# A tuned two-block language-model kernel: residual turns that transpose the tokens before they are normed

## The chip, the cores and the metric

The kernel is one program on one core of a Trainium2 chip. A core has a matrix engine (TensorE, PE in the profile; its weight loads are the row PEld), a vector engine (VectorE, DVE), an activation engine (ScalarE, ACT), GpSimd (POOL) and a queue engine that issues transfers (SyncE, SP). They share an on-chip memory (SBUF) and eight accumulation banks (PSUM, `bank[0]` to `bank[7]` in the code). Each engine works its own list in order and waits for the others on semaphores. The metric is the device time of one execution in microseconds (us), lower is better.

## The reference

256 tokens of width 1024 go through two blocks. What this change touches is in the second one:

```
def rms_norm(x, g):
    xf = xf * lax.rsqrt(jnp.mean(xf * xf, axis=-1, keepdims=True) + EPS)
    return (xf * g.astype(F32)).astype(x.dtype)

h = first_block(...)                   # ends: h + peer_ffn(...), then rmsnorm(h, g_final)
h = h + hgrn2_mixer(rms_norm(h, hg_norm), ...)      # q, f, i, g = split(x @ w_in, 4)
h = h + conv_ffn(rms_norm(h, ffn_norm[0]), ...)     # gate, val = split(x @ w_up, 2)
k, v = split(rms_norm(h, kv_norm) @ w_kv, 2)
h = h + swa_sink_attention(rms_norm(h, attn_norm), k, v, w_q, sinks, w_o)
h = h + conv_ffn(rms_norm(h, ffn_norm[1]), ...)
out = rms_norm(h, final_norm)
```

In the mixer q becomes `silu(q)`, f becomes `lower_bound + (1 - lower_bound) * sigmoid(f)`, k is one minus that, and eight levels of a gated linear attention follow. In the feed-forward, gate goes through a causal convolution over three tokens and a silu, and is multiplied with val. The norm's factor `rsqrt(mean(x*x) + EPS)` is one number for each token, its gain one number for each channel.

## The kernel before, in words

**Slabs.** All weights come as a stream of 524 slabs of 128 x 1024 floats. SP loads slab n into a ring of four (`RING = 4`). ACT rounds it to `whi` (L237, `split_hi`), DVE takes the rest `wlo = raw - whi` (L245, `split_lo`), both three slabs ahead (`AHEAD = 3`) of the slab that PE multiplies. Activations are split likewise into `xhi` and `xlo`, and a product is three matmuls (hi by hi, hi by lo, lo by hi). `up` (L273 to L275) multiplies a slab with the turned activations into one bank, 24 matmuls; `up_halves` (L294, L298) does it with eight wide and eight short ones; `down` (L338 to L340) adds 12 wide matmuls onto the residual banks 4 to 7; `up_wide` (L330 to L332) gives token-major outputs. An `up` into a bank waits (`up_evac`) until its last content has been taken out.

**A turn.** Between two layers stands a turn. `down_last` finishes the four residual banks one by one. DVE adds them to `h` (`add`, L510; `h` is token-major: two times 128 tokens by 1024). ACT squares each quarter with a sum (L624), takes the root (L637), DVE the reciprocal (L522), and `nt = h * factor` is written in pieces by DVE (`scale`, L527) and ACT (L661). PE turns `nt` by 16 transposes (`turn_pe`, L680 and L686). ACT reads the turned banks times the gain into `xhi` (`turn_hi`, L704), DVE into `xlo` (`turn_lo`, L713), in eight pieces each; the first `up` after the turn starts as soon as the first piece of `xlo` is there. There are six turns: T_WQ, T_HG (before the mixer, where the first block's final norm and the mixer's norm stand in a row, so that also `UT = h * g_final` is formed, L516), T_FF0, T_ATT, T_FF1 and T_OUT (the output).

**The mixer.** 16 `up`s in four banks give f (the first eight, taken out by ACT with a sigmoid, L2068) and q (the last eight: four taken out by DVE copies, L2226, four by ACT with a silu, L2082). DVE forms `forget` (L2179, L2182) and the residual (L2188), then scans the logarithms (L2233), subtracts (L2218) and forms differences (L2209, L2211). When all 16 are taken out (`up_evac`), PE may overwrite the banks with the token-major products (`up_wide`), between which the levels of the linear attention stand (L1979).

**The feed-forward.** For each of 22 tiles PE does an `up_halves` for the gate, one for val, and a `down`. Gate: ACT copies one half of its bank (L2396), DVE adds the other (L2439), ACT begins the convolution (L2399), DVE ends it (L2444). Val: ACT copy (L2404), DVE add (L2455), after the silu (L2407) DVE multiplies (L2458). The order of each engine's list is written out by hand; only SP and the ring decide when a slab arrives.

Of the kernel before, what the change touches and what calls it, by code (L numbers as in the profile page):

```python
# [131 lines left out]
def build(nc, t):  # L132
    ctx = ExitStack()
    with ctx:
# [148 lines left out]
        def up_halves(pe, n0, u0, i, r, U, uU=None, x_ready=None):  # L283
# [210 lines left out]
        TRT, TRS, TR1 = tiny[:, 42:44], tiny[:, 44:46], tiny[:, 46:48]  # L494
# [24 lines left out]
        def root_turned(dve, a, tt):  # L519

            dve.wait_ge(turn_rt, 2 * a + tt + 1)
            nc.vector.reciprocal(TRS[:, tt:tt + 1], TRT[:, tt:tt + 1]).then_inc(turn_rs, 1)  # L522
            dve.wait_ge(turn_rs, 2 * a + tt + 1)

        def scale(dve, a, c0, c1):
            src = UT if a == T_HG else h
            nc.vector.tensor_scalar(nt[:, c0:c1], src[:, c0:c1], TRS[:, c0 // D:c0 // D + 1], None, ALU.mult)\  # L527
                .then_inc(turn_nt, 1)
# [11 lines left out]
        def turn_dve(dve, a):  # L540
# [5 lines left out]
            if a == T_ATT:  # L546
                add(dve, a, 2)
                first_mean(dve, a)
                add(dve, a, 3)
                root_turned(dve, a, 0)  # L550
            else:
                first_mean(dve, a)
                add(dve, a, 2)
                root_turned(dve, a, 0)
                add(dve, a, 3)
# [7 lines left out]
        def mean_h(dve, tt, k0, k1, count):  # L563

            dve.wait_ge(turn_ss, SS_BASE[T_HG] + count)
            nc.vector.scalar_tensor_tensor(out=TW[:, tt:tt + 1], in0=ss(k0), scalar=EPS, in1=ss(k1),
                                           op0=ALU.add, op1=ALU.add).then_inc(turn_v, 1)

        def mean_u(dve, tt, k, count):

            dve.wait_ge(turn_ss, SS_BASE[T_HG] + count)
            dve.wait_ge(turn_v, V_BASE[T_HG] + 2 * tt + 1)
            nc.vector.scalar_tensor_tensor(out=TV[:, tt:tt + 1], in0=TW[:, tt:tt + 1], scalar=EPS, in1=ss(k),
                                           op0=ALU.mult, op1=ALU.add).then_inc(turn_v, 1)

        def turn_dve_gained(dve, row):

            a = T_HG  # L580
# [36 lines left out]

        def turn_act(act, a):
# [15 lines left out]
            def root(tt, k):
                act.wait_ge(turn_v, V_BASE[a] + VALUES[a] // 2 * (tt + 1))
# [4 lines left out]
            if a == T_HG:  # L640
                square(0, 0)
                square(1, 1)
                square_u(0, 2)
                square(2, 3)
                square_u(1, 4)
                root(0, 4)
                square(3, 5)
                square_u(2, 6)
                square_u(3, 7)
                root(1, 7)  # L650
            else:
                square(0, 0)
                square(1, 1)
                root(0, 1)
                square(2, 2)
# [2291 lines left out]
```

## Time and profile before

| | us |
|---|---|
| median of 3 runs | 1697.04 (1697.02 to 1697.94) |
| the profiled execution's own time | 1697.7 |
| its span in the profile | 1695.9 |
| PE busy | 1664.8 (98%) |
| DVE busy | 1286.7 (76%) |
| ACT busy | 1031.6 (61%) |

The profile is of one execution. Its engine rows count work, not waiting; what ends the program is read from the chain of waits and from which engine has no gaps. The engines' views in order of time show when an instruction started, how long it took, and in brackets how long its engine had been idle and who ended that.

### The profile page before, as it was taken

What the parts mean: (1) busy time and instruction counts of PE and PEld (TensorE: products, weight loads), DVE (VectorE), ACT (ScalarE), POOL (GpSimd) and SP (SyncE); (2) the same over time, 40 slices, a digit from 0 to 9 for tenths busy, and PEclk for the clock granted to TensorE, in tenths of its full rate; (3) what the DMA queues carried; (4) which work ended last, traced back from release to release, by engine and by line L of the source; (5) the groups of instructions that cost most, each with busy time, mean ns of one, the idle gap of its engine ahead of it and who ended that gap; (6) DMA issues with size and microseconds to landing.
All of it is one profiled execution on the core that took longest, in us unless ns stands there. A gap on an engine that the chain in (4) does not pass through costs nothing.

```text
span 1695.9 us, 34377 instructions
## 1 busy us (share of the span) xinstructions
PE 1664.8 (98%) x10835; PEld 1505.4 (89%) x10835; DVE 1286.7 (76%) x2365; ACT 1031.6 (61%) x1628; POOL 114.5 (7%) x102
## 2 busy tenths in 40 slices
PE   8999999999999999999999999999999999999998
PEld 7998889999999999988888888898888888878886
DVE  6866773899977777777777777789777777977776
ACT  7766655776556666654545455665576657766665
POOL 0024300344100000000000000100000000000000
PEclk9999999999999999999999999999999999999999
DMA  5543355777765555477787777542445564246563
GB/s 204 179 150 97 117 204 179 201 225 224 242 202 175 170 174 178 164 232 243 239 277 240 244 241 240 184 152 78 158 162 188 194 189 153 100 152 196 190 193 112
DMA packets 113405, 315.62 MB, mean 186 GB/s; under 512 B 12640, under 2 KB 44768, under 8 KB 112960
## 3 DMA queue, kind: packets, MB, share of 16 engines
q1 hardware_dynamic: 112032, 310.43, 56.5%
q0 software_dynamic: 848, 4.00, 0.7%
q8 instruction: 36, 0.59, 0.1%
q10 hardware_dynamic: 464, 0.40, 0.1%
q14 instruction: 25, 0.20, 0.0%
HBM read 296.43 MB, written 18.35 MB: 186 GB/s over the span
## 4 chain that ended last, share of the span: by engine, by line
PE 94%; DVE 2%; ACT 2%; issue 1%; DMA 1%; ACTq 0%; DVEq 0%; POOL 0%; POOLq 0%
PE bank L273 12%; PE bank L274 12%; PE bank L275 12%; PE bank L338 11%; PE bank L339 11%; PE bank L340 11%; PE bank L294 9%; PE bank L298 5%; PE bank L1522 3%; PE bank L1979 2%; PE bank L330 1%; PE bank L332 1%; PE bank L331 1%; DMA iota<-in_iota 1%; DVE h L510 0%
## 5 line engine op out<-in xcount | busy, mean ns | idle before, releaser
L245 DVE TENSOR_TENSOR wlo<-raw,whi 128x1024 fp32r<-128x1024 f32 x499 | 612.4, 1230 | 132.1 <-ACT whi L237 119.6
L237 ACT ACTIVATE whi<-raw 128x1024 fp32r<-128x1024 f32 x524 | 550.1, 1052 | 19.9 <-PE bank L332 14.0
L273 PE MATMUL bank<-x,whi 128*128 128x256 f32 (+1 forms) x1728 | 506.1, 293 | 1.5 <-DVE x L713 0.7
L275 PE MATMUL bank<-x,wlo 128*128 128x256 f32 (+1 forms) x1728 | 491.1, 284 | 0.0
L274 PE MATMUL bank<-x,whi 128*128 128x256 f32 (+1 forms) x1728 | 490.5, 284 | 0.0
L273 PEld LDWEIGHTS bank<-x,whi 128*128 128x128 f32 x1728 | 330.6, 191 | 5.2 <-issue 3.6
L274 PEld LDWEIGHTS bank<-x,whi 128*128 128x128 f32 x1728 | 331.3, 192 | 0.1
L275 PEld LDWEIGHTS bank<-x,wlo 128*128 128x128 f32 x1728 | 330.3, 191 | 0.0
L338 PE MATMUL bank<-whi,yhi 128*128 128x512 f32 x816 | 319.4, 391 | 0.8 <-DVE ylo L2319 0.7
L339 PE MATMUL bank<-wlo,yhi 128*128 128x512 f32 x816 | 318.2, 390 | 0.0
L340 PE MATMUL bank<-whi,ylo 128*128 128x512 f32 x816 | 317.6, 389 | 0.0
L338 PEld LDWEIGHTS bank<-whi,yhi 128*128 128x128 f32 x816 | 153.4, 188 | 33.5 <-issue 1.2
L340 PEld LDWEIGHTS bank<-whi,ylo 128*128 128x128 f32 x816 | 153.2, 188 | 32.4
L339 PEld LDWEIGHTS bank<-wlo,yhi 128*128 128x128 f32 x816 | 153.4, 188 | 29.4
L294 PE MATMUL bank<-x,whi 128*128 128x512 f32 x704 | 177.4, 392 | 0.9 <-DVE x L713 0.7
L1606 ACT ACTIVATE yhi<-h 128x256 fp32r<-128x256 f32 x128 | 53.4, 417 | 170.5 <-PE bank L340 167.1
L294 PEld LDWEIGHTS bank<-x,whi 128*128 128x128 f32 x704 | 129.2, 188 | 27.1 <-issue 1.2
L1559 ACT ACTIVATE h<-bank 128x256 f32<-128x256 f32 x128 | 49.0, 383 | 150.0 <-PE bank L275 149.7
L1800 DVE TENSOR_TENSOR ylo<-h,yhi 128x256 fp32r<-128x256 f32 x128 | 54.4, 425 | 66.5 <-ACT yhi L1606 66.3
L298 PEld LDWEIGHTS bank<-x,wlo 128*128 128x128 f32 x704 | 96.9, 190 | 6.9
L298 PE MATMUL bank<-x,wlo 128*128 128x256 f32 x704 | 100.2, 282 | 0.0
L1755 DVE TENSOR_SCALAR h<-iota,h 128x128 f32<-128x128 f32 x256 | 76.9, 343 | 22.9 <-PE bank L1522 22.9
(321 smaller groups left out, 1718.1 us busy)
## 6 DMA issues: line engine op xcount, KB each, us to landing
raw<-in_stream SPq DMA_DIRECT2D x524, 512.0 KB, 3.6
act_spill<-h SPq DMA_DIRECT2D x124, 128.0 KB, 3.3
h<-act_spill SPq DMA_DIRECT2D x124, 128.0 KB, 3.9
h<-in_x SPq DMA_DIRECT2D x2, 512.0 KB, 4.6
arena<-in_keys POOLq DMA_DIRECT2D x1, 1024.0 KB, 6.2
h_spill<-h SPq DMA_DIRECT2D x1, 1024.0 KB, 7.6
arena<-h_spill POOLq DMA_DIRECT2D x1, 1024.0 KB, 6.9
arena<-in_g_final POOLq DMA_DIRECT2D x1, 512.0 KB, 8.8
```

The lines of the kernel that those rows point to most:

```text
L237: nc.scalar.activation(whi[:, q * 1024:(q + 1) * 1024], raw[:, q * 1024:(q + 1) * 1024], ACT.Copy).then_inc(hi_ready, 1)
L245: nc.vector.tensor_tensor(wlo[:, q * 1024:(q + 1) * 1024], raw[:, q * 1024:(q + 1) * 1024], whi[:, q * 1024:(q + 1) * 1024].bitcast(F32), ...
L273: nc.tensor.matmul(bank[b][:, 0:T], whi[:, w], xhi[:, x], start=k == 0, stop=False)
L274: nc.tensor.matmul(bank[b][:, 0:T], whi[:, w], xlo[:, x], start=False, stop=False)
L275: last = nc.tensor.matmul(bank[b][:, 0:T], wlo[:, w], xhi[:, x], start=False, stop=k == KT - 1)
L294: return nc.tensor.matmul(bank[b][:, :], whi[:, w], both, start=k == 0, stop=k == KT - 1)
L298: return nc.tensor.matmul(bank[b][:, SEQ:2 * SEQ], wlo[:, w], xhi[:, k * SEQ:(k + 1) * SEQ], start=False, stop=stop, skip_group_check=True)
L338: nc.tensor.matmul(o, yhi[:, y], whi[:, w], start=first, stop=False, skip_group_check=True)
L339: nc.tensor.matmul(o, yhi[:, y], wlo[:, w], start=False, stop=False, skip_group_check=True)
L340: return nc.tensor.matmul(o, ylo[:, y], whi[:, w], start=False, stop=True, skip_group_check=True)
L1755: nc.vector.tensor_scalar(HOT1[:, y % 2 * P:(y % 2 + 1) * P], iota[:, :], c1(I1T), c1(GT_COLS), ALU.is_equal, ALU.mult).then_inc(s("hot_a" ...
L1800: nc.vector.tensor_tensor(ylo[:, yq * SEQ:(yq + 1) * SEQ], PRD[:, yq * SEQ:(yq + 1) * SEQ], yhi[:, yq * SEQ:(yq + 1) * SEQ].bitcast(F32), ...
```

## The change

At the four turns T_HG, T_FF0, T_ATT and T_FF1 PE now transposes `h` itself (`turn_pe_late`), as soon as the adds are done. The factor is worked out behind that (`factor_dve`, `roots_act`), and PE and ACT spread it to `ROW`, one number for each token, alike in all partitions (`row_pe`: two matmuls of the factor's column with the identity, `row_act`: a copy out of bank 7). It is applied where products are taken out: in the mixer all 16 `up`s are taken out by DVE as `bank * ROW` (`taken`), and ACT does sigmoid and silu in place behind that; v and the output gate get it as ACT's scale. In the feed-forward the gate is multiplied by `ROW` after its halves are added, val is left without the factor, and the down sums get it in the add of the next turn (T_ATT and T_OUT). In the attention keys are taken out by DVE times `ROW`, values get it in ACT's copy, and of the queries it goes into the scale of the exponential, so that the distance table and the sinks are divided by it. At T_HG the gain is the product of both norms' gains, for which `g_final` is loaded once more, channel-major.

```diff
+        def turn_dve_late(dve, a, gain_name, row=None):
+            add(dve, a, 0)
+            add(dve, a, 1)
...
+            add(dve, a, 3)
+            turn_lo(dve, a, gain_name)
+        def factor_dve(dve, a):
+            dve.wait_ge(turn_ss, SS_BASE[a] + SUMS[a])
...
+                nc.vector.reciprocal(INV, ROOT).then_inc(turn_rs, 1)
+        def turn_act_late(act, a, gain_name):
...
+            square(act, a, 2)
+            turn_hi(act, a, gain_name)
+        def row_pe(pe, a):
+            pe.wait_ge(turn_rs, R_BASE[a] + 1)
+            for tt in range(TT):
+                last = nc.tensor.matmul(bank[7][:, tt * P:(tt + 1) * P], INV[:, tt:tt + 1].to_broadcast([P, P]),
+                                        ident[:, :], start=True, stop=True)
+            last.then_inc(s("row_mm"), 1)
+        def row_act(act, a):
+            act.wait_ge(s("row_mm"), a - T_HG + 1)
+            nc.scalar.activation(ROW, bank[7][:, 0:SEQ], ACT.Copy).then_inc(s("row_ready"), 1)
+        def turn_pe_late(pe, a):
+            pe.wait_ge(h_done, 4 * a + 2)
+            for x in range(KT // 2):
+                for tt in range(TT):
+                    if tt and x in (0, KT // 4):
+                        pe.wait_ge(h_done, 4 * a + 3 + x // 2)
...
         def pe_hgrn(pe):
-            turn_pe(pe, T_HG)
+            turn_pe_late(pe, T_HG)
             up(pe, N_HG, U_HG, 0, 0, 4, SEQ, x_ready=lo_base(T_HG), banks=HG_BANKS)
-            steps(pe, 15, 4, lambda i, r: up(pe, N_HG + 1, U_HG + 1, i, r, 4, SEQ, banks=HG_BANKS))
+            up(pe, N_HG + 1, U_HG + 1, 0, 0, 4, SEQ, banks=HG_BANKS)
+            up(pe, N_HG + 2, U_HG + 2, 0, 0, 4, SEQ, banks=HG_BANKS)
+            row_pe(pe, T_HG)
+            steps(pe, 13, 4, lambda i, r: up(pe, N_HG + 3, U_HG + 3, i, r, 4, SEQ, banks=HG_BANKS))
         def act_hgrn(act, chain):
...
             for j in range(8):
-                split_hi(act, N_HG + j + AHEAD, 0, 0, 4)
-                act.wait_ge(slabs_done, N_HG + j + 1 + RING)
-                nc.scalar.activation(FG[:, j * SEQ:(j + 1) * SEQ], bank[(U_HG + j) % HG_BANKS][:, 0:SEQ], ACT.Sigmoid)\
-                    .then_inc(up_evac, 1)
+                if j > 1:
+                    split_hi(act, N_HG + j + AHEAD, 0, 0, 4)
+                act.wait_ge(up_evac, U_HG + j + 1 + 2)
+                f = slice(j * SEQ, (j + 1) * SEQ)
+                nc.scalar.activation(FG[:, f], FG[:, f], ACT.Sigmoid).then_inc(s("f_sig"), 1)
         def dve_hgrn(dve, chain):
...
+            def taken(j, out):
+                if j == 0:
+                    dve.wait_ge(s("row_ready"), 1)
+                dve.wait_ge(slabs_done, N_HG + j + 1 + RING)
+                nc.vector.tensor_tensor(out, bank[(U_HG + j) % HG_BANKS][:, 0:SEQ], ROW, ALU.mult)\
+                    .then_inc(up_evac, 1)
...
-                if j < 4:
-                    if j == 0:
-                        dve.wait_ge(up_evac, U_HG + 8 + 2)
-                    dve.wait_ge(slabs_done, N_HG + 8 + j + 1 + RING)
-                    nc.vector.tensor_copy(QQ[:, j * SEQ:(j + 1) * SEQ], bank[(U_HG + j) % HG_BANKS][:, 0:SEQ])\
-                        .then_inc(up_evac, 1)
+                taken(8 + j, QQ[:, j * SEQ:(j + 1) * SEQ])
         def dve_ffn(dve, f, chain):
...
-                nc.vector.tensor_tensor(gate, gate, bank[u % 2][:, 0:SEQ], ALU.add).then_inc(s("gate_sum"), 1)
+                nc.vector.tensor_tensor(gate, gate, bank[u % 2][:, 0:SEQ], ALU.add).then_inc(up_evac, 1)
+                dve.wait_ge(up_evac, u + i * 8 + 1 + 2)
+                if first:
+                    dve.wait_ge(s("row_ready"), a - T_HG + 1)
+                nc.vector.tensor_tensor(gate, gate, ROW, ALU.mult).then_inc(s("gate_sum"), 1)
```

**Where instructions move.** VectorE's list behind the adds of T_HG, before (L527 writes the normed tokens, L713 is `turn_lo`, L245 `split_lo`, L2166 to L2173 the lower bounds, L510 the last add, L516 the gain):

```order
L510 TENSOR_TENSOR h<-arena,bank 128x512
L516 TENSOR_TENSOR arena<-h,arena 128x512
L522 RECIPROCAL tiny<-tiny 128x1
L516 TENSOR_TENSOR arena<-h,arena 128x512
L566 SCALAR_TENSOR_TENSOR tiny<-tiny 128x1
L527 TENSOR_SCALAR arena<-arena,tiny 128x512
L573 SCALAR_TENSOR_TENSOR tiny<-tiny 128x1
L527 TENSOR_SCALAR arena<-arena,tiny 128x512
L522 RECIPROCAL tiny<-tiny 128x1
L527 TENSOR_SCALAR arena<-arena,tiny 128x256 x2
L713 SCALAR_TENSOR_TENSOR x<-bank,vec,x 128x256 x8
L245 TENSOR_TENSOR wlo<-raw,whi 128x1024
```

The same place in the changed kernel (L524 is the add, L751 `turn_lo`, L530 the gain, L591 to L599 the factor, L2230 `taken`):

```order
L524 TENSOR_TENSOR h<-arena,bank 128x512
L751 SCALAR_TENSOR_TENSOR x<-bank,tiny,x 128x256 x8
L530 TENSOR_TENSOR arena<-h,arena 128x512 x2
L245 TENSOR_TENSOR wlo<-raw,whi 128x1024 x2
L2213 TENSOR_TENSOR arena<-vec 128x8
L2214 TENSOR_TENSOR arena<-vec,arena 128x8
L2215 TENSOR_TENSOR arena<-vec,arena 128x8
L591 SCALAR_TENSOR_TENSOR tiny<-tiny 128x2
L594 SCALAR_TENSOR_TENSOR tiny<-tiny 128x2
L597 TENSOR_TENSOR tiny<-tiny 128x2
L599 RECIPROCAL tiny<-tiny 128x4
L2230 TENSOR_TENSOR arena<-bank,arena 128x256 x2
```

`turn_lo` now stands right behind the last add, and the factor, four instructions, stands behind two slab splits.

VectorE's list at the end of the mixer's 16 `up`s, before (L2226 is the last of its four copies, L2233 the scans, L2218 the subtraction, L2209 and L2211 the differences):

```order
L2226 COPY arena<-bank 128x256
L2233 SCALAR_TENSOR_TENSOR arena<-vec,arena 128x256 x8
L245 TENSOR_TENSOR wlo<-raw,whi 128x1024
L2218 TENSOR_TENSOR arena<-arena 128x2048
L245 TENSOR_TENSOR wlo<-raw,whi 128x1024
L2209 TENSOR_TENSOR arena<-arena 128x8x128
L2211 TENSOR_TENSOR arena<-arena 128x8x128
L245 TENSOR_TENSOR wlo<-raw,whi 128x1024
L2209 TENSOR_TENSOR arena<-arena 128x16x64
L2211 TENSOR_TENSOR arena<-arena 128x16x64
```

The same place in the changed kernel (L2289 the scans, L2279 the subtraction, L2270 and L2272 the differences):

```order
L2230 TENSOR_TENSOR arena<-bank,arena 128x256
L2289 SCALAR_TENSOR_TENSOR arena<-vec,arena 128x256 x8
L245 TENSOR_TENSOR wlo<-raw,whi 128x1024
L2279 TENSOR_TENSOR arena<-arena 128x2048
L2230 TENSOR_TENSOR arena<-bank,arena 128x256
L245 TENSOR_TENSOR wlo<-raw,whi 128x1024
L2270 TENSOR_TENSOR arena<-arena 128x8x128
L2272 TENSOR_TENSOR arena<-arena 128x8x128
L2230 TENSOR_TENSOR arena<-bank,arena 128x256
L245 TENSOR_TENSOR wlo<-raw,whi 128x1024
L2270 TENSOR_TENSOR arena<-arena 128x16x64
L2272 TENSOR_TENSOR arena<-arena 128x16x64
```

The last four products of q, which ACT took out before, now stand in VectorE's list between the scans, the subtraction and the differences.

ScalarE's list behind T_HG in the changed kernel (L742 is `turn_hi`, L627 and L634 the squares, L673 the root, L688 `row_act`, L2113 the exponential of the lower bounds, L2119 the sigmoid):

```order
L742 ACTIVATE x<-bank,tiny 128x256 x8
L237 ACTIVATE whi<-raw 128x1024
L627 ACTIVATE arena,tiny<-h 128x512
L634 ACTIVATE arena,tiny<-arena 128x512 x2
L237 ACTIVATE whi<-raw 128x1024
L634 ACTIVATE arena,tiny<-arena 128x512 x2
L673 ACTIVATE tiny<-tiny 128x4
L688 ACTIVATE arena<-bank 128x256
L237 ACTIVATE whi<-raw 128x1024
L2113 ACT_TABLE_LOAD
L2113 ACTIVATE arena<-arena 128x16
L2119 ACT_TABLE_LOAD
```

Before, all squares and the root stood ahead of `turn_hi`, a slab split stood between the exponential and the sigmoid's table load, and one behind each sigmoid; now two sigmoids follow that load before the next split.

## Rows read from the trace of the kernel before

**Rows 1.** The page: busy time of the engines, and the chain that ended last.

```profile
PE 1664.8 (98%) x10835; PEld 1505.4 (89%) x10835; DVE 1286.7 (76%) x2365; ACT 1031.6 (61%) x1628; POOL 114.5 (7%) x102
...
PE 94%; DVE 2%; ACT 2%; issue 1%; DMA 1%; ACTq 0%; DVEq 0%; POOL 0%; POOLq 0%
```

**Rows 2.** Waits of PE: who it waited for, us in total, times, longest.

```profile
PE bank L680 <- DVE arena L527: 9.6, 5, 3.2
```

**Rows 3.** Timeline, T_HG: start, us, engine, line, operation, [idle before <-releaser].

```profile
1069.32 0.39 PE L340 MATMUL bank<-whi,ylo 128*128 128x512 f32 x1
...
1070.23 0.68 DVE L510 TENSOR_TENSOR h<-arena,bank 128x512 f32<-128x512 f32 x1
...
1072.92 1.06 PE L680 MATMUL bank<-ident,arena 128*128 128x128 f32 x8 [3.21 <-DVE arena L527]
...
1074.57 3.02 ACT L704 ACTIVATE x<-bank,vec 128x256 fp32r<-128x256 f32 x8 [0.16 <-PE bank L686]
...
1075.70 0.55 PE L273 MATMUL bank<-x,whi 128*128 128x256 f32 x1
...
1077.69 0.28 PE L273 MATMUL bank<-x,whi 128*128 128x256 f32 x1
```

**Rows 4.** Windows at T_HG, T_FF0, T_ATT: PE, PEld, DVE, ACT, POOL busy; granted clock; DMA.

```profile
1074.00:1078.00 4.00, 3.91 (x20) 3.84 (x21) 3.01 (x9) 3.84 (x10) 0.00 (x0) 0.57 0.00 0
...
1229.00:1232.00 3.00, 1.91 (x15) 1.64 (x16) 1.97 (x7) 2.22 (x6) 0.00 (x0) 1.00 0.03 5
...
1418.00:1422.00 4.00, 3.23 (x17) 3.21 (x17) 2.52 (x10) 3.31 (x10) 0.54 (x1) 0.62 0.42 147
```

**Rows 5.** Timeline behind T_HG: ACT's table load and sigmoid, PE's pace.

```profile
1081.44 1.28 ACT L2068 ACT_TABLE_LOAD   x1
1082.73 0.39 ACT L2068 ACTIVATE arena<-bank 128x256 f32<-128x256 f32 x1
...
1085.44 0.39 ACT L2068 ACTIVATE arena<-bank 128x256 f32<-128x256 f32 x1 [0.15 <-PE bank L275]
...
1088.32 0.39 ACT L2068 ACTIVATE arena<-bank 128x256 f32<-128x256 f32 x1 [1.55 <-PE bank L275]
```

**Rows 6.** Window from the mixer's sigmoids to its first token-major product, columns as in Rows 4.

```profile
1081.50:1128.30 46.80, 46.44 (x368) 45.35 (x367) 38.24 (x52) 32.48 (x38) 0.00 (x0) 1.00 0.54 175
```

**Rows 7.** Timeline, end of the mixer's `up`s: DVE's scans, ACT's last silu, PE.

```profile
1112.37 4.76 DVE L2233 TENSOR_TENSOR_SCAN arena<-vec,arena 128x256 f32<-128x256 f32 x8
...
1122.88 0.38 ACT L2082 ACTIVATE arena<-bank 128x256 f32<-128x256 f32 x1 [1.55 <-PE bank L275]
1123.32 0.50 PE L330 MATMUL bank<-whi,x 128*128 128x512 f32 x1 [0.36 <-ACT arena L2082]
...
1128.31 0.15 DVE L2236 COPY arena<-bank 128x1 f32<-128x1 f32 x1
```

**Rows 8.** Timeline, T_FF0 up to the fourth product.

```profile
1228.15 0.39 PE L340 MATMUL bank<-whi,ylo 128*128 128x512 f32 x1
1228.64 0.69 DVE L510 TENSOR_TENSOR h<-h,bank 128x512 f32<-128x512 f32 x1 [0.38 <-PE bank L340]
...
1231.53 3.02 ACT L704 ACTIVATE x<-bank,vec 128x256 fp32r<-128x256 f32 x8
...
1232.66 0.47 PE L294 MATMUL bank<-x,whi 128*128 128x512 f32 x1 [0.37 <-DVE x L713]
...
1240.99 0.41 DVE L2455 TENSOR_TENSOR arena<-arena,bank 128x256 f32<-128x256 f32 x1
1241.66 2.00 PE L294 MATMUL bank<-x,whi 128*128 128x512 f32 x8
```

**Rows 9.** Timeline, a feed-forward tile in the loop: the gate's add.

```profile
1308.81 0.42 DVE L2439 TENSOR_TENSOR arena<-arena,bank 128x256 f32<-128x256 f32 x1 [0.94 <-ACT arena L2396]
```

**Rows 10.** Timeline, T_ATT: the second `turn_lo` and the product behind it.

```profile
1430.97 3.22 DVE L713 SCALAR_TENSOR_TENSOR x<-bank,vec,x 128x256 fp32r<-128x256 f32 x8
...
1431.60 0.36 PE L273 MATMUL bank<-x,whi 128*128 128x256 f32 x1 [0.29 <-DVE x L713]
```

More of the change, by code:

```diff
@@ L508, in add @@
             q = slice(p * 512, (p + 1) * 512)
+            if a in (T_ATT, T_OUT):
+                nc.vector.scalar_tensor_tensor(out=h[:, q], in0=bank[4 + p][:, :], scalar=INV[:, p // 2:p // 2 + 1],
+                                               in1=h[:, q], op0=ALU.mult, op1=ALU.add).then_inc(h_done, 1)
+                return
             old = H_OLD if a == T_HG else h
@@ L545, in turn_dve @@
             add(dve, a, 1)
[L546 to L555, printed above, removed]
+            first_mean(dve, a)
+            add(dve, a, 2)
+            root_turned(dve, a, 0)
+            add(dve, a, 3)
             scale(dve, a, 0, D // 2)
@@ L639, in turn_act @@
             nc.scalar.activation(tiny[:, 20 + a:21 + a], tiny[:, 31:32], ACT.Sqrt)
[L640 to L655, printed above, removed]
-                square(3, 3)
-                root(1, 3)
@@ L658, in turn_act @@
-            act.wait_ge(turn_rs, 2 * a + 2)
+            square(act, a, 0)
+            square(act, a, 1)
+            root(0, 1)
+            square(act, a, 2)
+            square(act, a, 3)
+            root(1, 3)
+            act.wait_ge(turn_rs, R_BASE[a] + 2)
             if a == T_OUT:
                 act.wait_ge(turn_u, 4 + 1)
-            nc.scalar.activation(nt[:, D + 512:2 * D], (UT if a in (T_HG, T_OUT) else h)[:, D + 512:2 * D], ACT.Copy,
+            nc.scalar.activation(nt[:, D + 512:2 * D], (UT if a == T_OUT else h)[:, D + 512:2 * D], ACT.Copy,
@@ L2055, in act_hgrn @@
         def act_hgrn(act, chain):
-            turn_act(act, T_HG)
-            turn_hi(act, T_HG, "hg_norm")
+            act.wait_ge(s("hg_gain"), 1)
+            turn_act_late(act, T_HG, HG_GAIN)
             split_hi(act, N_HG - 1 + AHEAD, 0, 0, 4)
-            nc.scalar.activation(TR1[:, 0:1], TW[:, 0:1], ACT.Sqrt)\
-                .then_inc(s("x2_rt"), 1)
-            nc.scalar.activation(TR1[:, 1:2], TW[:, 1:2], ACT.Sqrt)\
-                .then_inc(s("x2_rt"), 1)
+            square(act, T_HG, 3)
+            square_u(act, 0)
+            square_u(act, 1)
+            split_hi(act, N_HG + AHEAD, 0, 0, 4)
+            square_u(act, 2)
+            square_u(act, 3)
+            roots_act(act, T_HG)
+            row_act(act, T_HG)
+            split_hi(act, N_HG + 1 + AHEAD, 0, 0, 4)
             act.wait_ge(s("lb_x"), 2)
@@ L2581, in act_attn @@
         def act_attn(act, chain):
-            turn_act(act, T_ATT)
-            turn_hi(act, T_ATT, "kv_norm")
+            turn_act_late(act, T_ATT, "kv_norm")
+            square(act, T_ATT, 3)
+            roots_act(act, T_ATT)
             split_hi(act, N_ATT - 1 + AHEAD, 0, 0, 4)
-            for k in range(2):
+            row_act(act, T_ATT)
+            for k in range(3):
                 split_hi(act, N_ATT + k + AHEAD, 0, 0, 4)
-                act.wait_ge(slabs_done, N_ATT + k + 1 + RING)
-                nc.scalar.activation(KTA[:, k * SEQ:(k + 1) * SEQ], bank[(U_ATT + k) % 2][:, 0:SEQ], ACT.Copy)\
-                    .then_inc(up_evac, 1)
-            split_hi(act, N_ATT + 2 + AHEAD, 0, 0, 4)
             turn_hi(act, T_ATT, "attn_norm", 1)
+            act.wait_ge(up_evac, U_ATT + 2 + 2)
             nc.scalar.activation(VD, bank[(U_ATT + 2) % 2][:, 0:SEQ], ACT.Copy).then_inc(up_evac, 1)
```

283 lines of the change are left out of this document (167 added, 116 removed).

## The prediction

> **What bounds the kernel now.** I read the page's busy row and the chain first: PE is busy 1664.8 of 1695.9 us, and 94% of the chain is PE [rows 1]. So a microsecond counts only where PE stops or slows. The waits of PE came second: few are left, and the largest, 9.6 us in five, is PE's transposes waiting for DVE's scaled tokens in a turn [rows 2]. Third, the timeline of each turn. At T_HG the last down matmul starts at 1069.32, the transposes at 1072.92 after 3.21 us idle, the first product at 1075.70 [rows 3]; at T_FF0 it is 1228.15 and 1232.66 [rows 8]. Fourth, the granted clock in these windows: 0.57 behind T_HG, 0.62 at T_ATT, 1.00 at T_FF0, where PE had idled less [rows 4]; a share near a half is the 1.2 GHz level instead of 2.4. Last, and this decides for me, what DVE and ACT do in the 50 us behind a turn, since the change takes work out of the turn and puts it there.
>
> **Turns, what goes.** PE needs only the adds. At T_FF0 PE is free at 1228.4. Sixteen transposes at 0.13 us (eight take 1.06, rows 3) take 2.1 us; the last add starts at 1228.64 and takes 0.69 [rows 8], and ten transposes cover it. So they end at 1230.5. ACT's `turn_hi` starts 0.37 after the third begins (1231.16 to 1231.53 before), at 1229.0 instead of 1231.53. The first product stood 1.13 behind it and would at 1230.1, but the transposes hold it to 1230.55: 2.1 us earlier than 1232.66. T_FF1 has the same form. At T_HG the gain pieces keep the last add near 1069.9 to 1070.6 (0.68, rows 3), the transposes end at 1071.65, and the first product starts at 1071.7, 4.0 us earlier. With no 3 us of idling ahead the slow clock should go too; before, the first nine product matmuls took from 1075.70 to 1077.69 [rows 3], where nine at 0.12 each take 1.08, so 0.9 more. At T_ATT the same steps give 1419.7 against 1422.0, 2.3. The four together: 4.9 + 2.1 + 2.3 + 2.1 = 11.4 us. That is what the turns offer, if nothing behind them is late.
>
> **T_FF0 and T_FF1, what is late next.** The fourth product (val of the second tile) may start only when DVE has taken the second out (L2455). Before, that was 1240.99 plus 0.41, and the product started at 1241.66 [rows 8]: no room. Now DVE does, from the end of `turn_lo` at 1233.05: the factor (0.16, ACT's root 0.3, the reciprocal 0.16 and the handovers, 0.75 in all; ACT's last square lies beside it), a split whose `whi` ACT ends at 1234.6 (to 1235.8), the gate's add (0.4), a wait on itself and the product with `ROW` (0.55), a split (to 1238.3, ACT's `row_act` is ahead of its `whi`), the convolution (1.0), a split (1.15) and the val add (0.4): 1240.9. PE is ready at 1239.3 (two row matmuls, 0.3, included), stands 1.6 us, and starts at 1240.95. Of 2.1 us 0.7 stay. Bounds: 0 and 2.1. I take 0.7, since each piece has a row's duration.
>
> **T_ATT.** In the last tile before it ACT's `whi` split now falls ahead of the val copy, so the last adds come 0.3 later; I included that. Behind it DVE takes out two key products (0.4 each) that ACT took, after waiting for `ROW`. The second `turn_lo` then starts at 1430.3, where it started at 1430.97 and PE followed at 1431.60 [rows 10]: 0.6 to 0.7 us stay, taken 0.6. Bounds: -0.5 (the small scalings of table and sinks, six instructions of 0.15 to 0.3, get in the way) and 2.3.
>
> **In the feed-forward loop** each of 44 tiles has one more DVE instruction of 0.42 and a wait on itself, 0.55 us. DVE waits 0.94 us in each tile for the next gate [rows 9], so it is hidden: 0. If that cover were gone it would be up to 0.1 to 0.2 a tile, 4 to 8 us. T_OUT: an add with a factor for an add; `turn_lo` of the same kind takes 0.40 for 256 columns as the plain add does, so 0.1 at most.
>
> **The mixer, first half.** PE at its pace of 2.88 us an `up` (1085.44 to 1088.32, rows 5) ends the third at 1080.4; the factor is there at 1080.3 (DVE: last split to 1078.5, lower bounds, four small ones, ACT's root), so `row_pe` costs only its 0.3. But the sixth `up` needs its slab split, and on ACT in front of that stand now `row_act` (to 1081.4), a split (1082.45), the exponential's load 1.28 and 0.2, the sigmoid's load 1.28, two sigmoids at 0.39, then the split: 1087.0, and DVE's part 1088.25. PE wants it at 1086.7: it stands 1.6 us. PE is then at 1088.3 where it was at 1090.9.
>
> **The mixer, its end.** PE may begin the token-major products only when all 16 products are taken out. Before, ACT did the last at 1122.88 and PE began at 1123.32 after 0.36 us, while DVE was still 5 us behind with scans, subtraction and differences, up to 1128.31 [rows 7]. Now the last four stand in that list of DVE's. From the scans' start the list is 1128.31 - 1112.37 = 15.9 us, and four more at 0.38 make 17.5. The scans' start: DVE is busy without a gap from 1087.1 to 1103.3 (six splits 6.8, five products 1.9, eight pairs of `forget` 5.3, residual 1.4, lower bounds 0.8), then waits for splits behind ACT's logarithms; I get 1110.9 against 1112.37. So the last product is out at 1128.3 and PE begins at 1128.5 instead of 1123.3: 5.2 later than before, the turn's gain used up. PE has stood over 7 us by then, and starts at the lower clock. Behind T_HG it lasted from 1074.1 to 1077.5 [rows 3, 4]: at half pace 1.7 us lost. Together +6.9.
> Bounds. Below: DVE is busy 38.24 us in the 46.8 up to 1128.3 [rows 6]; less one split (1.14) that now comes sooner, plus lower bounds 0.8, plus twelve products at 0.38, it is 42.5. Begun at 1081.5, when `ROW` is there, and without one wait, it ends at 1124.0, 0.7 after 1123.3, and with the clock +2.4. Above: the scans no earlier than before, +6.7, and the clock over 4 us, +2: about +8.7. I take 6.9, for DVE stood 8.6 of these 46.8 us, nearly all of it waiting for ACT's splits, and ACT's list gets no shorter.
> From there to T_FF0 PE was without gaps and DVE some microseconds ahead; PE coming later keeps DVE ahead.
>
> ACT's table loads weigh in this. The row shows the load 1.28 us and the sigmoid starting right behind it, at 1082.73 [rows 5]. The Trainium skill, ScalarE: Activation LUTs, What ACT_TABLE_LOAD costs, adds a drain of about 1.38 us to each load's 1.28. By that rule the sixth `up` would wait 2.8 us longer and the scans come later by about 1.4, and the sum would be some 1.4 us higher; by the row it is as above, and the row decides.
>
> **The sum.** +6.9 - 0.7 - 0.6 - 0.7 + 0.1 = +5.0 us. The profiled execution took 1697.7 (span 1695.9), so 1702.7; the median of the runs is 1697.04, 0.66 lower, so I say 1702.0.
>
> **Rivals.**
> (a) The evictions fit and all the turns keep their gain: -11.4 + 4 times 0.3 for the rows, -10.2, 1686.8. For it: ACT is idle 14.3 of 46.8 us there [rows 6], and PE waits for next to nobody there now. Against it: DVE's 42.5 us. 8%.
> (b) The mixer's end comes out near its lower bound (+2.4) and the later turns keep 1 to 1.5 each: -1, 1696. It needs ACT's `whi` to be ready whenever DVE asks. 26%; two thirds of these lie within 0.2%, a sixth on each side.
> (c) The forecast, the last four evictions queue behind the scans: 58%, 1699.5 to 1706.
> (d) Slower still: the loop's 0.94 us is no real cover, since the self-wait and the later convolution delay ACT's splits too. It decides from the point where the tile's chain passes 8.3 us; at 0.15 a tile +6.6 on top, 1708.6. 8%.
>
> Faster by over 0.2% (3.4 us, about what a measurement of this kernel tells from none): (a) and some of (b), 0.13. Within: most of (b) and the low edge of (c), 0.19. Slower: 0.68. The range, 1694 to 1707, leaves out (a) and (d); for (c) alone it is 1699.5 to 1706.
>
> **What would show it.** In the timeline after: no idle of over 1.5 us between the last down matmul and the first product of a turn, and a granted clock of 1.00 there; a stop of 1 to 2 us ahead of the sixth `up`; PE idle 5 to 8 us ahead of the first token-major product, released by DVE's product with `ROW`, and a granted clock near a half behind it; 1 to 2 us of PE idle ahead of the fourth product of each feed-forward; DVE's idle ahead of the gate's add down from 0.94 to about 0.4. I am wrong if PE enters the token-major products before 1124, or if PE has gaps in the feed-forward loop.

## The result, and the profile after

The changed kernel takes 1708.06 us (median of 4 runs, 1706.95 to 1708.9), the one before, run beside it, 1697.18 (4 runs, 1697.02 to 1697.94): a ratio of 1.0063, 95% interval 1.0048 to 1.0078. It is slower, as forecast, but by 10.9 us and not by 5.0, and the time lies outside the range. The profiled execution took 1706.95 with a span of 1705.2, against 1697.7 and 1695.9: 9.3 more in the trace.

First the page. TensorE's busy time is to the tenth that of [rows 1], while VectorE's is 18.6 us higher.

```profile
PE 1664.8 (98%) x10851; PEld 1505.5 (88%) x10851; DVE 1305.3 (77%) x2404; ACT 1028.2 (60%) x1620; POOL 115.4 (7%) x103
```

Then the waits of PE (who it waited for, us in total, times, longest). The 9.6 us of [rows 2] are down to 1.3 (T_WQ, which keeps its old form) and 0.6 for adds. One large wait is new, and three small kinds: ahead of the fourth product of each feed-forward (1.4 each), at the second `turn_lo` of T_ATT (1.5, where it was 0.3) and ahead of the sixth `up` (1.4).

```profile
PE bank L332 <- DVE arena L2230: 12.6, 1, 12.6
...
PE bank L294 <- DVE arena L2522: 2.8, 2, 1.4
...
PE bank L273 <- DVE x L751: 1.8, 2, 1.5
PE bank L273 <- DVE wlo L245: 1.4, 1, 1.4
PE bank L705 <- DVE arena L540: 1.3, 1, 1.3
```

The turn T_HG in the timeline (start, us, engine, line, operation). Last down matmul at 1068.89, transposes right behind it, first product at 1070.80: 1.91 us, where [rows 3] had 6.38. The turn does what the change says.

```profile
1068.89 0.39 PE L342 MATMUL bank<-whi,ylo 128*128 128x512 f32 x1
1069.12 1.92 PE L723 MATMUL bank<-ident,h 128*128 128x128 f32 x16
1070.80 0.36 PE L273 MATMUL bank<-x,whi 128*128 128x256 f32 x1
```

The windows at T_HG, T_FF0 and T_ATT, columns as in [rows 4]: the granted clock (third from the right) is 1.00, the 2.4 GHz level, at all three.

```profile
1069.00:1075.00 6.00, 5.96 (x49) 5.65 (x48) 5.73 (x13) 6.00 (x16) 2.17 (x2) 1.00 0.67 262
1230.00:1240.00 10.00, 10.00 (x47) 8.07 (x46) 6.66 (x9) 6.70 (x13) 0.00 (x0) 1.00 0.64 210
1428.00:1440.00 12.00, 11.44 (x90) 10.85 (x90) 9.21 (x18) 10.15 (x25) 0.54 (x1) 1.00 0.41 125
```

Where the 9.3 us of the trace come from can be read by laying the last down matmul of each turn beside that of before. The stretch from T_HG to T_FF0 lasts 170.55 us (1068.89 to 1239.44), where it lasted 158.83: +11.7. The first feed-forward gives back 0.7, attention 0.9, the second feed-forward 0.6; the end adds 0.2, and the stretch up to T_HG, which the change does not touch, was 0.4 shorter. So the loss is in the mixer alone. The timeline of VectorE at its end, against [rows 7]:

```profile
1109.67 4.76 DVE L2289 TENSOR_TENSOR_SCAN arena<-vec,arena 128x256 f32<-128x256 f32 x8
1114.34 1.20 DVE L245 TENSOR_TENSOR wlo<-raw,whi 128x1024 fp32r<-128x1024 f32 x1
1115.46 2.29 DVE L2279 TENSOR_TENSOR arena<-arena 128x2048 f32<-128x2048 f32 x1
1117.66 0.42 DVE L2230 TENSOR_TENSOR arena<-bank,arena 128x256 f32<-128x256 f32 x1
1120.37 1.23 DVE L245 TENSOR_TENSOR wlo<-raw,whi 128x1024 fp32r<-128x1024 f32 x1 [2.29 <-ACT whi L237]
...
1123.78 0.42 DVE L2230 TENSOR_TENSOR arena<-bank,arena 128x256 f32<-128x256 f32 x1
1125.62 1.22 DVE L245 TENSOR_TENSOR wlo<-raw,whi 128x1024 fp32r<-128x1024 f32 x1 [1.43 <-ACT whi L237]
...
1129.04 0.42 DVE L2230 TENSOR_TENSOR arena<-bank,arena 128x256 f32<-128x256 f32 x1
1130.88 1.23 DVE L245 TENSOR_TENSOR wlo<-raw,whi 128x1024 fp32r<-128x1024 f32 x1 [1.43 <-ACT whi L237]
1132.03 0.42 DVE L2230 TENSOR_TENSOR arena<-bank,arena 128x256 f32<-128x256 f32 x1
```

and that of ScalarE in the same stretch:

```profile
1109.43 1.28 ACT L2131 ACT_TABLE_LOAD   x1
1118.11 1.27 ACT L2131 ACTIVATE arena<-arena 128x1280 f32<-128x1280 f32 x1 [7.40 <-DVE arena L2230]
1119.29 1.04 ACT L237 ACTIVATE whi<-raw 128x1024 fp32r<-128x1024 f32 x1
1124.23 0.42 ACT L2131 ACTIVATE arena<-arena 128x256 f32<-128x256 f32 x1 [3.90 <-DVE arena L2230]
1124.55 1.04 ACT L237 ACTIVATE whi<-raw 128x1024 fp32r<-128x1024 f32 x1
```

Read the two together. ScalarE's silu (L2131) stands ahead of its next split (L237) and waits for VectorE's taken (L2230); VectorE's next split of the low half (L245) waits for that split; and the next taken stands behind it. The engines pass the work to and fro, each idle meanwhile: VectorE 2.29 + 1.43 + 1.43 = 5.15 us. TensorE, done with its last `up` and a transpose by 1119.9, waits for all of it:

```profile
1119.61 0.27 PE L2027 MATMUL bank<-ident,arena 128*128 128x128 f32 x1
1132.50 0.80 PE L332 MATMUL bank<-whi,x 128*128 128x512 f32 x1 [12.62 <-DVE arena L2230]
```

The windows of this stretch (columns as before) show the granted clock at 0.50, the 1.2 GHz level, by 1128, while TensorE stands, and on until after 1136:

```profile
1122.00:1128.00 6.00, 0.00 (x0) 0.00 (x0) 4.57 (x6) 1.36 (x2) 0.00 (x0) 0.62 0.29 89
1128.00:1132.00 4.00, 0.00 (x0) 0.00 (x0) 2.57 (x3) 1.36 (x2) 0.00 (x0) 0.50 0.38 128
1132.00:1136.00 4.00, 3.50 (x8) 2.82 (x9) 0.51 (x3) 3.49 (x4) 0.00 (x0) 0.50 0.41 131
1136.00:1140.00 4.00, 4.00 (x16) 3.21 (x15) 2.71 (x3) 3.40 (x5) 0.00 (x0) 0.86 0.10 15
```

The first half of the mixer and the two feed-forwards came as forecast: one stop ahead of the sixth `up`, one ahead of the fourth product, and VectorE's idle ahead of the gate's sum at 0.42 to 0.63 in the loop, where [rows 9] had 0.94.

```profile
1087.84 0.38 PE L273 MATMUL bank<-x,whi 128*128 128x256 f32 x1 [1.38 <-DVE wlo L245]
...
1252.34 2.08 PE L294 MATMUL bank<-x,whi 128*128 128x512 f32 x8 [1.41 <-DVE arena L2522]
...
1302.96 0.42 DVE L2501 TENSOR_TENSOR arena<-arena,bank 128x256 f32<-128x256 f32 x1 [0.63 <-ACT arena L2454]
```

### The profile page after: what moved, and what is told of

The parts are those of the page before. It is cut to its first block, busy times and chain, and to the rows that moved or that the text cites. A ratio compares the mean times of both kernels' runs of the same rounds, so it can differ in the third digit from the quotient of the medians.

```text
span 1705.2 us, 34469 instructions
## 1 busy us (share of the span) xinstructions
PE 1664.8 (98%) x10851; PEld 1505.5 (88%) x10851; DVE 1305.3 (77%) x2404; ACT 1028.2 (60%) x1620; POOL 115.4 (7%) x103
## 4 chain that ended last, share of the span: by engine, by line
PE 90%; DVE 5%; ACT 2%; issue 1%; DMA 1%; ACTq 0%; DVEq 0%; POOL 0%; SPq 0%; POOLq 0%
PE bank L273 11%; PE bank L274 11%; PE bank L275 11%; PE bank L340 11%; PE bank L341 10%; PE bank L342 10%; PE bank L294 9%; PE bank L298 5%; PE bank L1560 3%; PE bank L2023 2%; DVE wlo L245 1%; PE bank L332 1%; PE bank L334 1%; PE bank L333 1%; ACT whi L237 1%
## 5 line engine op out<-in xcount | busy, mean ns | idle before, releaser
L245 DVE TENSOR_TENSOR wlo<-raw,whi 128x1024 fp32r<-128x1024 f32 x499 | 612.6, 1230 | 138.9 <-ACT whi L237 129.0
L237 ACT ACTIVATE whi<-raw 128x1024 fp32r<-128x1024 f32 x524 | 549.4, 1050 | 18.8 <-PE bank L334 15.6
```

The costliest lines, as they stand in the source:

```text
L237: nc.scalar.activation(whi[:, q * 1024:(q + 1) * 1024], raw[:, q * 1024:(q + 1) * 1024], ACT.Copy).then_inc(hi_ready, 1)
L245: nc.vector.tensor_tensor(wlo[:, q * 1024:(q + 1) * 1024], raw[:, q * 1024:(q + 1) * 1024], whi[:, q * 1024:(q + 1) * 1024].bitcast(F32), ...
```

## The experiments

Each kernel was timed in five rounds beside the kernel before, whose median was 1697.18 us (22 runs) beside the first four, 1697.10 (25) beside the next four and 1697.10 (15) beside the last. The ratios are to it.

| kernel | us, median | runs | ratio to before, 95% interval |
|---|---|---|---|
| e1, silus behind the splits | 1702.46 | 7 | 1.0032, 1.0020 to 1.0043 |
| e2, e1 and takens early on VectorE | 1693.13 | 10 | 0.9975, 0.9966 to 0.9985 |
| e3, TensorE kept busy in the wait | 1706.21 | 5 | 1.0054, 1.0041 to 1.0068 |
| e4, mixer as before | 1695.58 | 11 | 0.9988, 0.9979 to 0.9997 |
| e7, takens early, silus left | 1694.14 | 11 | 0.9985, 0.9976 to 0.9994 |
| e6, e2 and one split ahead | 1691.92 | 10 | 0.9972, 0.9963 to 0.9981 |
| e8, e2 and two more multiplications a tile | 1701.33 | 10 | 1.0022, 1.0013 to 1.0032 |
| e9, e6 and the value sum ahead of a split | 1690.36 | 5 | 0.9961, 0.9947 to 0.9975 |
| e10, e2 and one more multiplication a tile | 1693.87 | 11 | 0.9979, 0.9970 to 0.9988 |

**e1: the silus behind the splits.** In `act_hgrn`:

```diff
             for j in range(8):
                 split_hi(act, N_HG + 8 + j + AHEAD, 0, 0, 4)
...
-                if j >= 4:
-                    q = slice(0, 5 * SEQ) if j == 4 else slice(j * SEQ, (j + 1) * SEQ)
-                    act.wait_ge(up_evac, U_HG + 8 + j + 1 + 2)
-                    nc.scalar.activation(QQ[:, q], QQ[:, q], ACT.Silu)...
+            for j in range(4, 8):
+                (the same four calls)
```

> Only ScalarE's order changes: the four silu calls on the columns of Q come behind the last of the eight splits instead of between them. Theory A (of the 12.6 us that TensorE waits ahead of the token-major products, 5.15 us is VectorE idle, 2.29 + 1.43 + 1.43, waiting for a split that stands behind a silu that waits for VectorE's own taken): those three idle pieces go, the wait falls to about 7.4 us, the time to about 1702.9 us. Theory B (VectorE's added work is the bound, the idle pieces only move elsewhere): the wait stays above 11 us and the time within 1 us of 1708.1.

1702.46 us, 5.6 under the changed kernel. In the timeline VectorE runs from the scans (1110.84) to the end of the last taken (1128.20) without a gap, 17.4 us, and PE's wait is 7.19. Theory A holds, B falls. The clock still goes to its half behind the wait, for a shorter time: the first of these windows is wholly at the half, the second at 0.99.

```profile
1128.25 0.79 PE L332 MATMUL bank<-whi,x 128*128 128x512 f32 x1 [7.19 <-DVE arena L2230]
```

```profile
1128.00:1132.00 4.00, 3.75 (x9) 2.98 (x10) 0.26 (x2) 3.75 (x5) 0.00 (x0) 0.50 0.43 131
1132.00:1136.00 4.00, 4.00 (x21) 3.36 (x20) 2.96 (x3) 3.79 (x5) 0.00 (x0) 0.99 0.09 24
```

**e2: the takens ahead of work that nobody waits for yet.** As e1, and in `dve_hgrn` behind the scans:

```diff
-            (split, subtraction, taken 12; split, differences(0), taken 13;
-             split, differences(1), taken 14; split, taken 15; copy of ONC)
+            split_lo(dve, N_HG + 12 + AHEAD, 0, 0, 4)
+            taken(12, QQ[:, 4 * SEQ:5 * SEQ])
+            nc.vector.tensor_tensor(CKN, CUM, CKN, ALU.subtract)...
+            split_lo(dve, N_HG + 13 + AHEAD, 0, 0, 4)
+            for j in (5, 6, 7):
+                taken(8 + j, QQ[:, j * SEQ:(j + 1) * SEQ])
+            nc.vector.tensor_copy(ONC, bank[7][:, 0:1])...
+            (split, differences(0), split, differences(1))
```

> As the first, and on VectorE the four last takens (and the copy of the out norm's column) are written ahead of the third split and of both differences, in place of one behind each. Theory A (the late start of the token-major products is a matter of order, not of work added): TensorE's wait ahead of them falls to about 1 us, the clock stays at 1.00 there, VectorE is done with the differences near 1127.3 us as in the kernel before, and the time is about 1694 us, 3 under the kernel before. Theory B (VectorE's work is the bound): the level stage takes the wait over and the time is not under 1701 us.

1693.13 us, 9.3 under e1 and 4.1 under the kernel before. The three takens stand together, PE waits 0.41, and the clock is 1.00 throughout the layer. VectorE's second pair of differences ends at 1126.20, 58.2 us behind the last down matmul of T_HG; in the kernel before it ended at 1127.25, 57.9 us behind it. So VectorE is as late as it was, though it has taken out four products more and nobody waits for it.

```profile
1118.22 1.10 DVE L2230 TENSOR_TENSOR arena<-bank,arena 128x256 f32<-128x256 f32 x3
...
1124.98 1.22 DVE L2272 TENSOR_TENSOR arena<-arena 128x1024 f32<-128x1024 f32 x1
```

```profile
1119.38 0.50 PE L332 MATMUL bank<-whi,x 128*128 128x512 f32 x1 [0.41 <-DVE arena L2230]
```

The same instructions in another order: so the loss of the change was order, not work.

**e3: TensorE busy in the wait.** In `pe_hgrn`, ahead of the wait:

```diff
+            for _ in range(48):
+                nc.tensor.matmul(bank[6][:, :], xhi[:, 0:P], xhi[:, 0:512], start=True, stop=True)
             pe.wait_ge(up_evac, U_HG + 16 + 2)
```

> 48 matmuls of 128x512 whose result is not used stand on TensorE in the 12.6 us wait ahead of the token-major products; at the full clock they take about 11 us, so they end before the wait does. Theory A (2.2 us of the loss is that TensorE runs its first products behind the wait at half its clock): the granted clock stays at 1.00 and the time falls by 2.2 us to about 1705.9. Rival: VectorE's late end sets the level stage anyway, the products' slow start is hidden behind it, and the time stays at 1708.1.

1706.21 us, 1.85 under the changed kernel. The filler ran 11.14 us and the products behind it start as late as before, at 1132.64, but at the full clock (1.00 in every window from 1108 to 1142): from there to the last down of T_FF0 (1237.45) it is 104.8 us; in the changed kernel 106.9, in the kernel before 104.8 (1123.32 to 1228.15). The slow clock costs 2.1 us, and is not hidden.

```profile
1119.78 11.14 PE L2029 MATMUL bank<-x 128*128 128x512 f32 x48
1132.64 0.50 PE L332 MATMUL bank<-whi,x 128*128 128x512 f32 x1 [1.72 <-DVE arena L2232]
```

**e4: the other three turns alone.** The hunks of the change in `turn_*_late` stay for T_FF0, T_ATT and T_FF1; `pe_hgrn`, `act_hgrn`, `dve_hgrn` and the turn T_HG are those of before:

```diff
-            turn_pe_late(pe, T_HG)
+            turn_pe(pe, T_HG)
...
-            turn_dve_late(dve, T_HG, HG_GAIN, G_FINAL)
+            turn_dve_gained(dve, G_FINAL)
+            turn_lo(dve, T_HG, "hg_norm")
```

> The turn into the mixer and the whole mixer layer as in the kernel before; the other three turns transpose unnormed tokens. Theory A (the whole loss is in the mixer layer, and the other three turns pay 0.7, 0.9 and 0.6 us, less 0.1 to 0.2 at the end): 1695.2 us, 2.0 under the kernel before. Rival C (the late turns do not pay by themselves, the feed-forward's added multiplication takes it back): 1697 us or more.

1695.58 us, 1.6 under the kernel before where 2.0 was expected; the interval, 0.9979 to 0.9997 of it, is 0.5 to 3.6 us. The three turns pay, by little; the stretches of its trace say the same, 0.7, 0.9 and 0.6 us less, and 0.2 more at the end. Against e2, which adds the late turn of the mixer with the order mended, it is 2.45 us slower: of the 4.9 us that the prediction saw in T_HG about half is kept.

**e7: must both lists change?** e2's VectorE list with the changed kernel's ScalarE list.

> VectorE's list as in e2 (the last takens ahead of the third split and the differences), ScalarE's as in the changed kernel (the silus between the splits). Theory A (a silu stands in the way only while the taken that it waits for comes late): within 1 us of e2, 1693 to 1694 us. Rival (both lists must change, the silus hold the splits up all the same): 1697 us or more, with VectorE idle for splits between 1115 and 1128 us.

1694.14 us: VectorE's order alone gives back 13.9 of the 15 us between the changed kernel and e2. The silus in between cost about 1 us, little more than the medians can tell; in the trace the stretch from T_HG to T_FF0 is 0.9 us longer than in e2, with one idle piece of 0.70 ahead of a split and a new wait of TensorE, 0.46, among the levels:

```profile
1120.44 1.23 DVE L245 TENSOR_TENSOR wlo<-raw,whi 128x1024 fp32r<-128x1024 f32 x1 [0.70 <-ACT whi L237]
...
1136.84 3.81 PE L2023 MATMUL bank<-arena 128*128 128x128 f32 x32 [0.46 <-DVE arena L2317]
```

**e6: the stop ahead of the sixth `up`.** e2, and in `act_hgrn`:

```diff
             split_hi(act, N_HG + 1 + AHEAD, 0, 0, 4)
+            split_hi(act, N_HG + 2 + AHEAD, 0, 0, 4)
             act.wait_ge(s("lb_x"), 2)
             nc.scalar.activation(LBE, LBE, ACT.Exp)...
             for j in range(8):
-                if j > 1:
+                if j > 2:
                     split_hi(act, N_HG + j + AHEAD, 0, 0, 4)
```

> e2, and ScalarE's split of the third slab of the mixer stands ahead of the exponential and sigmoid calls with their two table loads. Theory A (the 1.38 us stall ahead of the sixth up goes, and since TensorE sets the pace from there to the scans, all behind it comes as much earlier): about 1691.8 us. Rival (VectorE's scans start when they did, the stall was hidden): 1693.1 us.

1691.92 us, 1.2 under e2. The wait on `wlo` is gone from PE's list, and the stretch from the first transposes of T_HG (1068.95) to those of T_FF0 (1224.04) is 155.1 us against 156.2 in e2 (1068.21 to 1224.43). Not all of the stop's 1.38 us is won: the wait ahead of the token-major products is 0.96, where e2 had 0.41.

**e8 and e10: how much cover has the feed-forward loop?** e2, and in `dve_ffn`, with 2 or 1 for n:

```diff
                 dve.wait_ge(up_evac, u + i * 8 + 1 + 2)
...
+                for e in range(n):
+                    nc.vector.tensor_tensor(MORE[:, (2 * e + b) * SEQ:(2 * e + b + 1) * SEQ], gate, ROW, ALU.mult)
                 nc.vector.tensor_tensor(gate, gate, ROW, ALU.mult).then_inc(s("gate_sum"), 1)
```

> e2, and VectorE does two more multiplications of 128x256 in every tile of both feed-forwards, at the place of the one that the change added; their results are not used. Cost of each 0.42 us, together 0.8 us, against the 0.63 us for which VectorE still waits ahead of the gate's sum. Theory A (the loop's cover is those 0.63 us and no more): about 0.2 us for each of some 40 tiles, 1700 us. Rival (VectorE has more room, as its busy share of 0.77 in the loop suggests: 1.9 us of 8.3 idle): 1693 to 1694 us.

1701.33 us, 8.2 over e2. The number is near the expectation and its reason is wrong: between the fourth product and the last tile no product waited. The one added wait is at the last tile's down:

```profile
1308.73 0.76 DVE L2513 TENSOR_TENSOR arena<-arena 128x256 f32<-128x256 f32 x2
...
1407.91 0.41 DVE L2508 TENSOR_TENSOR arena<-arena,bank 128x256 f32<-128x256 f32 x1
```

```profile
1413.27 0.47 PE L340 MATMUL bank<-whi,yhi 128*128 128x512 f32 x1 [2.42 <-DVE ylo L2539]
```

```profile
1400.00:1418.00 18.00, 15.58 (x72) 12.66 (x71) 14.74 (x27) 11.71 (x22) 0.00 (x0) 0.91 0.57 171
```

In e2 the last gate's sum starts 179.5 us behind the first transpose of T_FF0, in e8 182.1 (1407.91 less 1225.84). VectorE's first tiles take 7.6 us in e2, where TensorE's take 8.31, and so it gets ahead; in e8 its tiles take 8.3 from the start, and it has no lead at the end, where the last down must wait for its own tile. Each feed-forward has that wait, and is 4.5 to 4.7 us longer in all (first transposes to the last down matmul of the next turn: 191.4 and 191.6 us, against 186.9 twice in e2); the clock, 0.91 over the 18 us of the window at the end of the first, can make about 1.6 us of the rest (an estimate, 0.09 of 18). Attention behind the first gives 1.1 us back: 82.0 from last down to last down, against 83.1 in the changed kernel.

> As e8 with one more multiplication instead of two. In e8 no product in the loop waited: VectorE's list merely lost the lead that it has on TensorE (2.6 us at the last tile), and the cost fell at the last tile of each feed-forward, as a 2.4 us wait and a slow clock behind it. Theory A' (the cover of the loop is that lead, built up where VectorE's tiles are shorter than TensorE's 8.31 us; with one more 0.34 us its list still gains on TensorE): 1693 to 1694 us, as e2. Rival (the added work costs by its length wherever it stands, half of e8's 8.2 us): 1697 us.

1693.87 us, 0.7 over e2, far from the rival's 1697; the last tile's sum starts at 179.5 again (1404.61 less 1225.09), and the wait at the last down is not there. Both are of one account: VectorE's tile is 7.6 us in e2, 7.9 in e10 and 8.3 in e8, against TensorE's 8.31. While it is shorter, VectorE gains a lead and then stands idle for the rest of each tile (0.63 in e2, 0.29 in e10); once it is as long, no lead is built, and the price falls at the end of the loop. One more instruction fits, two do not. What a tile clearly longer than 8.31 us would cost was not run.

```profile
1404.61 0.42 DVE L2508 TENSOR_TENSOR arena<-arena,bank 128x256 f32<-128x256 f32 x1 [0.21 <-ACT arena L2461]
```

**e9: the fastest.** e6, and in the first tile of each feed-forward:

```diff
-                if not last:
+                if not last and not first:
                     split_lo(dve, n + 1 + AHEAD, i, 0, 12)
...
                 nc.vector.tensor_tensor(y, y, bank[(u + 1) % 2][:, 0:SEQ], ALU.add).then_inc(up_evac, 1)
+                if first:
+                    split_lo(dve, n + 1 + AHEAD, i, 0, 12)
```

> e6, and in the first tile of each feed-forward VectorE's sum of the value half stands ahead of its split. Theory A (TensorE's wait of 1.41 us ahead of the fourth product, once in each feed-forward, is that split's 1.1 us and little else): 2.2 us under e6, about 1689.6 us. Rival (the next product waits for the split instead): as e6.

1690.36 us, 1.6 under e6 where 2.2 was expected, and 6.7 under the kernel before (ratio 0.9961, 0.9947 to 0.9975). PE's wait ahead of the fourth product is 0.27; the stretch of the first feed-forward is 0.9 us shorter (186.0 against 186.9), that of the second, from its first product, 1.0 (184.3 against 185.3), and the rest of the gap to 2.2 lies within what the medians tell.

```profile
1236.46 2.06 PE L294 MATMUL bank<-x,whi 128*128 128x512 f32 x8 [0.27 <-DVE arena L2529]
```

## Why the prediction was wrong, step by step

- **The turns.** Right in the mechanism, a little low in the sum. The first product comes 1.91 us behind the last down matmul at T_HG (6.38 before), 1.90 at T_FF0 and T_FF1 (4.51 before) and 3.20 at T_ATT (5.96 before), and the clock stays at its upper level: 4.5, 2.6, 2.6 and 2.8 us earlier, where the forecast had 4.0, 2.1, 2.1 and 2.3. The slow clock behind T_HG was priced at 0.9. From the last down of T_HG to the first token-major product it is 54.00 us in the kernel before and 53.53 in e4, which has the same turn at the full clock: 0.5. The 4.9 for T_HG is met because the two errors cancel.
- **T_FF0, T_FF1, "of 2.1 us 0.7 stay".** 0.7 and 0.6 are left, but of 2.6: the stall (1.41 for 1.6) and the row matmuls take the rest, 0.5 more than forecast, which is what the turn gained more. The stall is the one that was forecast, and e9 shows by moving it that the split in front of the val add is nearly the whole of it.
- **T_ATT, 0.6.** 0.9 by the trace. Same mechanism: of the 2.8 us won at the turn, TensorE's wait at the second `turn_lo` takes 1.2 back (1.46 where it was 0.29).

```profile
1441.01 0.35 PE L273 MATMUL bank<-x,whi 128*128 128x256 f32 x1 [1.46 <-DVE x L751]
```

- **The loop, 0.** Right in the number; e10 confirms it. But "DVE waits 0.94 us in each tile, so it is hidden" names only the sign of the cover: in e8 VectorE has no idle time left ahead of any gate's sum, no tile in the loop is late, and 8.2 us are lost all the same. Rival (d)'s "point where the tile's chain passes 8.3 us" is about where e8 stands, but the price falls once, at the last tile.
- **The mixer, first half.** Right: 1.38 us ahead of the sixth `up` for 1.6. ScalarE's rows are those that were used: load and call without a gap.

```profile
1081.96 1.28 ACT L2113 ACT_TABLE_LOAD   x1
1083.25 0.22 ACT L2113 ACTIVATE arena<-arena 128x16 f32<-128x16 f32 x1
```

  The Trainium skill, ScalarE: Activation LUTs, What ACT_TABLE_LOAD costs, adds a drain of about 1.38 us to each load; by it the stop would have been over 4 us (an estimate, two drains on the 1.38 measured), and the trace does not agree: the call starts 0.01 us behind the load's end.
- **The mixer, its end: here it failed.** The step was "from the scans' start the list is 15.9 us, and four more at 0.38 make 17.5", to begin at 1128.5, 5.2 later. Counted from the last down of T_HG, PE began its token-major products 63.6 us behind, where it was 54.0: 9.6 later. The scans started at 1109.67, 1.2 earlier than forecast (0.4 of it from ahead of T_HG); the list then took 22.8 us (to 1132.45) instead of 17.5, 5.15 of it idle. I had lengthened VectorE's list by its own instructions alone. The 15.9 us were measured while ScalarE's silus read the banks themselves and waited only for TensorE. In the new list each silu waits for a taken, and the next split for the silu: a wait in both directions between two lists. The order of both lists was there to be read; I added up the durations on one of them. e1 takes exactly this away: its list is 17.4 us, its stretch from T_HG to T_FF0 5.9 us over the kernel before where 6.9 was forecast, and its 1702.46 us are near the 1702.0 forecast for the change. In effect I had priced e1. Those 5 us were a matter of order too, as e2 shows, and e7 shows that VectorE's order alone breaks the circle.
- **The clock, 1.7.** 2.1, by e3. The mechanism was right and the size 0.4 low. In e1, behind the shorter wait, the slow stretch ended at 1132, in the changed kernel it lasted until after 1136.
- **The bounds.** The upper one, +8.7 for this term, was worked out with "the scans no earlier than before" as the worst case, again of one list. The term measured +11.7.
- **Rival (d), 1708.6.** The measured 1708.06 lies beside it by luck: its mechanism, tiles of the loop that come late, is not there, and both feed-forwards are shorter than before.

By the stretches of the trace: 11.7 - 0.7 - 0.9 - 0.6 + 0.2 = +9.7, less 0.4 from ahead of T_HG, is the 9.3 of the spans. The forecast had 6.9 - 0.7 - 0.6 - 0.7 + 0.1 = 5.0. Of the difference in the sum, 4.7, the one term makes 4.8 and all others together -0.1.

Of what T_HG offers e2 keeps only about half (2.45 of 4.9 us by the medians of e2 and e4). The traces account for most of it. Behind the last down of T_HG the first product of e2 comes 4.36 us earlier than in e4, the first token-major product 2.13 earlier; between them lie the stop ahead of the sixth `up` (1.38) and the row matmuls (0.36 of TensorE's time). The last 0.5 us were not traced to an instruction.

## What to carry to other kernels

When an eviction moves from one engine to another, don't lengthen one engine's list by the moved work: write the two lists side by side and follow every wait that now crosses between them. Two engines whose lists each hold an item that waits for the other's last item run one after the other, however idle both look. And an item that releases a third engine, the one that bounds, belongs ahead of work that nobody waits for yet: moving four evictions of 0.4 us past a subtraction, two splits and two pairs of differences was worth more here (9.3 us) than the whole change had hoped for in that layer.

## What the runs showed of the hardware

- TensorE's clock after standing still. In a wait of 12.6 us the granted clock fell to 0.50, and it stayed there behind the wait's end (1132.50) until after 1136; behind one of 7.2 us, ended at 1128.25, it was 0.50 to 1132 and 0.99 from there; with matmuls in the wait (e3) it stayed at 1.00. Behind the same 3.21 us of idling at T_HG it was 0.57 in the kernel before [rows 4] and 1.00 in e4, whose turn there is the same code. So the slow clock behind a stop of 3 us, which the prediction took as sure, came in one of these two profiled executions and not in the other.

```profile
1073.61 1.06 PE L790 MATMUL bank<-ident,arena 128*128 128x128 f32 x8 [3.21 <-DVE arena L541]
```

```profile
1074.00:1078.00 4.00, 3.47 (x26) 2.77 (x24) 2.91 (x9) 3.72 (x10) 0.00 (x0) 1.00 0.08 31
```

- The granted clock fell to 0.5 for a few microseconds near 127 us from the span's start in the profiled executions of before, e1, e4 and e9, and not in those of the changed kernel, e2, e3, e6, e7, e8 and e10, in code that none of the experiments touches. The last down matmul of T_HG started at 1069.32 to 1070.07 in the four with the dip and at 1067.98 to 1069.46 in the seven without. So a difference of 1 to 2 us between two single executions can lie ahead of everything that was changed; a stretch between two points of one trace leaves it out.
